# Input and memory handed over in both layouts, one column block for index keys, low rank and head weights, router in column groups

## The chip, the cores and the metric

The kernel runs on one core of one Trainium2 chip. The metric is the device time of one execution in microseconds; of several executions the median is taken. The core has TensorE (PE, matrix products; PEld is its weight load), VectorE (DVE), ScalarE (ACT), GpSimd (POOL) and SyncE (SP), which here issues nearly all DMAs.

## The reference, cut to what matters

A decoder trunk of two layers on 256 tokens of 1024 features, with a memory of 256 tokens, all float32. `hn` is RMSNorm of the stream `h`.

```
z = hn @ W_in[i]                        # 2616 columns, cut into the groups below
(a_q, a_k, a_v, a_g, a_lr, b_u, c_q, c_k, c_v, c_qi, c_ki, c_wi, d_uv) = split_cols(z, IN_SPLITS)
# widths: 128 128 256 256 16 256 256 256 256 256 32 8 512
o_a: gated linear attention;  logit = a_lr @ wa2 + ba        (a_lr: 16 columns, the low rank)
o_b: causal pooling of b_u
o_c: sparse attention; score = sum_h relu(c_qi_h . c_ki) * c_wi_h, top 64 of the visible tokens
     (c_ki: 32 columns, the index key; c_wi: 8 columns, one weight per index head)
o_d: chunked gating of d_uv
h += concat(o_a, o_b, o_c, o_d) @ W_out[i]
h += cross_attention(RMSNorm(h), RMSNorm(mem)) # keys and values from mem @ wkv, gain norm_mem
h += SwiGLU(RMSNorm(h))                        # layer 0
h += top-2-of-8 SwiGLU experts                 # layer 1: logits = RMSNorm(h) @ router (1024 x 8)
```

One final RMSNorm ends it.

## The kernel before, in words

Everything is written out by hand: one instruction list for each engine, ordered by semaphores. There is no planner. Each engine runs its list in order, so whatever stands behind a waiting instruction on the same engine waits too. One `for layer in range(2)` loop in each list holds the layer; the expert stage comes behind it.

**Weights.** Seven ring slots of 2 MB (`ring`) hold the weights. They are packed on the host into the order in which they are used, and SP issues one DMA per unit as soon as the slot's semaphore `slot_free` says that PE is done with what was there. `IN_UNITS` names the seven column blocks of `W_in`: unit `U_QI` holds index queries, index keys and head weights (296 columns), `U_A` the first 512 columns, `U_AG` the gate and the low rank (272 columns). Then `U_CQ`, `U_CV`, `U_BU`, `U_UV` follow, and after them `wkv`, `W_out` in four parts, `wq` and `wo`.

**Features on partitions.** PE contracts over the partitions, so the normalised stream is needed transposed, as `xnT` (128 partitions, 8 feature tiles, 256 tokens). `transposes()` (line 1574) gets it by 16 float32 products of `h` with `diag`, a diagonal matrix of 1/rms that DVE makes in `factors()` (lines 1014, 1015); each product shows as two records in the profile. `normed_out()` on DVE (line 1023) and ACT (line 690) then copies PSUM to `xnT` times the gain, which stands in `pcol`, one column per tile. `pcol` is itself made each layer: eight small DMAs fill `prow` (lines 517 to 521), PE transposes it (line 1633) and ACT copies it (line 723). The memory goes the same way in layer 0: `memr` (which lies in `memT`) is squared by ACT, multiplied with `diag` by PE, and copied back to `memT`.

**The start of a layer on PE.** Transposes of `h`; index queries (two column tiles of 128, `on_features`, line 1588, 8 products of 256 tokens each); index keys (32 columns, one more such group); head weights on tokens (`on_tokens`, line 1593: 8 products for each of two token tiles with 8 moving columns); in layer 0 the bias product (line 1649); in layer 0 three filler products (`keep_busy`, line 1560), in layer 1 the first column tile of `U_A`; the index scores `dots(1, 256)` (line 1658, eight products in four row groups); in layer 0 the transposes of the memory and three more fillers; transposes of `wsr` (line 1676); `U_A` (lines 1588, 1593); in layer 0 two products for the relative bias (line 1693) from `hank`, which comes back from DRAM by a DMA that POOL issues (line 620); `dots(0, 128)`; the low rank (16 columns, 8 products, line 1588); the gate on tokens (line 1593); then `U_CQ`, the `logit` product (line 1713) between its two halves, and the rest of the units.

**DVE in the same stretch.** After `xnT`: masks `wsr`, copies `qiT`, in layer 0 makes the memory's factors and half of the copies, then `score_and_take(1, 256)` and `score_and_take(0, 128)`: eight multiply-adds each (line 1092) and eight rounds of maximum and replace (lines 1099, 1100). Only behind these stands the copy `lrT` of the low rank (line 1067), for which the `logit` product waits.

**The router.** After the last update of `h` in layer 1 PE turns `h` by 16 products with the identity (line 1990), ACT and DVE scale it (lines 865, 1355), PE forms the logits of 8 experts in one accumulation of 8 products (line 1997), ACT copies them, two transposes (line 2002) bring them on tokens, and DVE makes the choice. The expert stage then streams 2 MB units through ring slots and two extra buffers; the first units are loaded ahead while the router runs.

Of the kernel before, what the change touches and what calls it, by code (L numbers as in the profile page):

```python
# [8 lines left out]
P = 128  # L9
# [4 lines left out]
ALU = mybir.AluOpType  # L14
# [50 lines left out]
def packed_blocks():  # L65

    for layer in range(DEPTH):
        for s, (lo, hi) in enumerate(IN_UNITS):
            yield ("in_units", layer, s), "w_in", layer, (0, D), (lo, hi)
        yield ("wkv", layer), "xa_wkv", layer, (0, D), (0, 2 * GW)  # L70
        for i, m in enumerate(WOUT_ORDER):
            yield ("wout", layer, i), "w_out", layer, (256 * m, 256 * m + 256), (0, D)
        yield ("wq", layer), "xa_wq", layer, (0, D), (0, GW)
        yield ("wo", layer), "xa_wo", layer, (0, GW), (0, D)
    for c, n in enumerate(FFN_TILES):
        f0 = P * sum(FFN_TILES[:c])
        for w, name in enumerate(("ffn_w1", "ffn_w3")):
            yield ("ffn", 3 * c + w), name, 0, (0, D), (f0, f0 + n * P)
        yield ("ffn", 3 * c + 2), "ffn_w2", 0, (f0, f0 + n * P), (0, D)
# [7 lines left out]

def pack_weights(inputs):

    return np.concatenate([rows_on_partitions(inputs[name][index, r0:r1, c0:c1])  # L90
                           for _, name, index, (r0, r1), (c0, c1) in packed_blocks()])

def pack_experts(inputs):
# [11 lines left out]
    return out  # L106

# [63 lines left out]
IN_UNITS = ((C_QI, C_UV), (0, 512), (C_AG, C_BU), (C_CQ, C_CV), (C_CV, C_QI), (C_BU, C_CQ), (C_UV, IN_W))  # L171
# [10 lines left out]
for _key, _, _, (_r0, _r1), (_c0, _c1) in packed_blocks():  # L182
    PACKED[_key] = (_at, _at + (_r1 - _r0) * (_c1 - _c0))
    _at = PACKED[_key][1]
# [4 lines left out]

CONST = {}  # L190
_at = 0
for _name, _w in (("ident", P), ("vis", 256), ("reset", 256), ("bd", 256), ("tril", P), ("inv", 512),
                  ("before", P), ("ones", P), ("iota", P), ("eidx", 8), ("erev", 8), ("limit", 16)):
# [5 lines left out]
def shape_constants():  # L199
# [21 lines left out]
    put("erev", 8 - np.arange(8)[None, :])  # L221
    put("limit", np.concatenate(([SMALL], np.full(N_EXP - 1, SMALL - 1), [SMALL + P], np.full(N_EXP - 1, P)))[None, :])
# [14 lines left out]
def build(nc, A, out):  # L237
    ctx = ExitStack()
    with ctx:
# [76 lines left out]
        wa2 = sb("wa2", [GLA_RANK, P])  # L316
        prow = sb("prow", [N_ROWS, P])
        pcol = sb("pcol", [P, N_ROWS])
# [47 lines left out]
        memr = memT[:, :, :].rearrange("p k m -> p (k m)").rearrange("p (t d) -> p t d", t=2)  # L366
# [7 lines left out]
        lrT = qidx[0:GLA_RANK, 768:1024]  # L374
# [1865 lines left out]
```

## Time and profile before

| | us |
|---|---|
| median of 3 runs | 1389.37 (1389.14 to 1391.38) |
| profiled execution | 1391.46 |
| its span | 1389.7 |
| PE busy | 1286.5 (93%) |
| DVE busy | 484.4 (35%) |
| ACT busy | 373.7 (27%) |
| POOL busy | 79.9 (6%) |
| moved by DMA | 433.51 MB, 312 GB/s over the span |

The profiled execution took 2.1 us more than the median. The profile of it has several views: the busy time of the engines in slices, the chain of work that ended last (each piece is what the next one had waited for), the instructions in order of time, groups of instructions by line, and the DMA issues with the time to landing.
### The profile page before, as it was taken

Reading aid. Unit: us, or ns where it says so; the run is one execution under the profiler, and the core shown is the slowest. Engines: PE = TensorE matmul, PEld = TensorE weight load, DVE = VectorE, ACT = ScalarE, POOL = GpSimd, SP = SyncE. Lnnn points to the kernel's source line nnn. Section 1 sums busy time; section 2 is a strip of 40 time slices with the busy share of each in tenths; the row PEclk is TensorE's granted clock in tenths of the full one; section 3 lists DMA queues with packets and bytes.
Section 4 is the critical chain, followed back from the end, with each engine's and each line's share of the span. In section 5 each row is a group of like instructions: output and inputs, shape, how many; then the busy total and the mean of one; then the engine's idle time right before and its main releaser. Section 6 shows DMA issues by size and latency. Waiting matters only on the chain.

```text
span 1389.7 us, 15762 instructions
## 1 busy us (share of the span) xinstructions
PE 1286.5 (93%) x6338; PEld 785.7 (57%) x6338; DVE 484.4 (35%) x819; ACT 373.7 (27%) x574; POOL 79.9 (6%) x68
## 2 busy tenths in 40 slices
PE   7999999999999999999989879779779778999996
PEld 5777888888888688634323224224224225788532
DVE  1627267777626453600101001001001004988102
ACT  2244154444323423301101001001001005776102
POOL 0263000000004600000000000000000000000000
PEclk9999999999999999999999999999999999999998
DMA  9431633443181308799999999999999999999895
GB/s 361 177 116 37 231 133 137 177 186 137 40 352 65 117 1 365 306 417 428 427 428 426 429 428 430 428 428 427 430 429 428 429 427 430 427 428 379 365 428 244
DMA packets 37416, 433.51 MB, mean 312 GB/s; under 512 B 5726, under 2 KB 7924, under 8 KB 9588
## 3 DMA queue, kind: packets, MB, share of 16 engines
q1 hardware_dynamic: 37172, 432.25, 75.4%
q8 instruction: 37, 0.61, 0.2%
q0 software_dynamic: 192, 0.53, 0.1%
q14 instruction: 15, 0.12, 0.0%
HBM read 431.71 MB, written 1.05 MB: 311 GB/s over the span
## 4 chain that ended last, share of the span: by engine, by line
PE 62%; DMA 32%; DVE 4%; ACT 1%; issue 1%; SPq 0%; DVEq 0%; ACTq 0%
DMA ring<-in_experts 31%; PE bank L2089 10%; PE bank L2169 9%; PE bank L1588 8%; PE bank L1975 6%; PE bank L1593 5%; PE bank L2099 5%; PE bank L1611 4%; PE bank L1979 3%; PE bank L1574 1%; PE bank L1865 1%; PE bank L1866 1%; PE bank L1872 1%; PE bank L2022 1%; PE bank L2047 1%; PE bank L1560 1%
## 5 line engine op out<-in xcount | busy, mean ns | idle before, releaser
L2089 PE MATMUL bank<-ring,xs 128*64 128x512 f32 x1552 | 352.1, 597 | 41.2 <-DMA ring<-in_experts 41.2
L2089 PEld LDWEIGHTS bank<-ring,xs 128*64 128x64 f32 x1552 | 109.6, 137 | 247.9 <-issue 228.4
L2099 PE MATMUL bank<-ring,s_act 128*64 128x512 f32 x768 | 176.3, 597 | 34.5 <-DMA ring<-in_experts 34.3
L1477 DVE TENSOR_TENSOR s_act<-wsT,bank 128x256 f32<-128x256 f32 x49 | 20.6, 421 | 510.8 <-ACT wsT L903 510.8
L2099 PEld LDWEIGHTS bank<-ring,s_act 128*64 128x64 f32 x768 | 55.6, 137 | 142.8 <-issue 131.4
L1975 PE MATMUL bank<-x_both,wf_hi 128*128 128x512 f32 x336 | 118.9, 396 | 0.0
L903 ACT ACTIVATE wsT<-bank 128x256 f32<-128x256 f32 x49 | 18.8, 383 | 336.3 <-PE bank L2047 336.3
L1588 PE MATMUL bank<-xnT,ring 128*128 128x256 f32 (+2 forms) x448 | 102.5, 388 | 0.6 <-ACT bias L752 0.6
L1501 DVE TENSOR_TENSOR ring_lo<-ring,w_hi 128x2048 fp32r<-128x2048 f32 (+1 forms) x44 | 96.0, 2193 | 20.2 <-ACT w_hi L960 20.2
L838 ACT ACTIVATE wf_hi<-ring 128x1024 fp32r<-128x1024 f32 x66 | 69.8, 1060 | 98.6 <-PE bank L1975 67.5
L1979 PE MATMUL bank<-x_both,wf_lo 128*128 128x256 f32 x336 | 94.1, 280 | 0.0
L1272 DVE TENSOR_TENSOR wf_lo<-ring,wf_hi 128x1024 fp32r<-128x1024 f32 x66 | 80.5, 1223 | 33.4 <-ACT wf_hi L838 33.4
L1588 PEld LDWEIGHTS bank<-xnT,ring 128*128 128x128 f32 (+2 forms) x448 | 80.5, 182 | 18.5 <-issue 2.1
L960 ACT ACTIVATE w_hi<-ring 128x2048 fp32r<-128x2048 f32 (+1 forms) x44 | 80.7, 1839 | 34.6 <-PE bank L2169 29.8
L899 ACT ACTIVATE j_act<-bank 128x512 f32<-128x512 f32 x49 | 29.3, 597 | 191.4 <-PE bank L2089 191.4
L1593 PE MATMUL bank<-ring,xnT 128*128 128x256 f32 (+2 forms) x320 | 78.5, 400 | 0.0
L2169 PE MATMUL bank<-w_hi,xg 128*128 128x512 f32 x224 | 72.8, 402 | 2.6 <-DVE xg L1508 2.6
L1975 PEld LDWEIGHTS bank<-x_both,wf_hi 128*128 128x128 f32 x336 | 63.1, 188 | 14.9
L1593 PEld LDWEIGHTS bank<-ring,xnT 128*128 128x128 f32 x320 | 56.4, 193 | 20.9 <-issue 16.0
L1979 PEld LDWEIGHTS bank<-x_both,wf_lo 128*128 128x128 f32 x336 | 63.5, 189 | 0.9
L2169 PEld LDWEIGHTS bank<-w_hi,xg 128*128 128x128 f32 x224 | 42.9, 192 | 13.7 <-issue 3.5
L2047 PEld LDWEIGHTS bank<-cst,j_act 128*128 128x128 f32 x224 | 24.0, 141 | 40.9 <-issue 40.1
(361 smaller groups left out, 1459.8 us busy)
## 6 DMA issues: line engine op xcount, KB each, us to landing
ring<-in_experts SPq DMA_DIRECT2D x166, 2048.0 KB, 29.2
ring<-in_packed SPq DMA_DIRECT2D x18, 1536.0 KB, 6.9
ring<-in_packed SPq DMA_DIRECT2D x11, 2048.0 KB, 10.2
ring<-in_packed SPq DMA_DIRECT2D x16, 1024.0 KB, 4.9
extra<-in_experts SPq DMA_DIRECT2D x2, 2048.0 KB, 11.8
ring<-in_packed SPq DMA_DIRECT2D x2, 1184.0 KB, 6.1
ring<-in_packed SPq DMA_DIRECT2D x2, 1088.0 KB, 10.9
h<-in_x SPq DMA_DIRECT2D x2, 512.0 KB, 4.0
```

The lines of the kernel that those rows point to most:

```text
L838: act.activation(as_piece(w, ffn_hi(i)), weights, ACT.Copy).then_inc(S["hi_ready"], 1)
L960: act.activation(w_hi[:, i % NB, 0:hi - lo], ring[:, slot, lo:hi], ACT.Copy)\
L1272: dve.tensor_tensor(as_piece(w, ffn_lo(i)), weights, as_piece(w, ffn_hi(i)), sub)\
L1501: dve.tensor_tensor(ring_lo[slot][:, lo:hi], ring[:, slot, lo:hi], w_hi[:, i % NB, 0:hi - lo], sub).then_inc(S["lo_ready"], 1)
L1588: i = mm(dst, w[:, k, :], src[:, k, :], start=k == 0, stop=k == KT - 1)
L1593: i = mm(dst, src[:, k, P * t:P * t + P], w[:, k, :], start=k == 0, stop=k == KT - 1)
L1611: ins = mm(dst, x, y, start=opens and n % 3 == 0, stop=closes and n % 3 == 2)
L1975: ins = mm(dst[:, :], wh[:, k, :], x_both[:, k, :], start=k == 0, stop=False, skip_group_check=True)
L1979: ins = mm(dst[:, 0:SEQ], wl[:, k, :], x_both[:, k, 0:SEQ], start=False, stop=k == KT - 1, skip_group_check=True)
L2089: i = mm(ps[d % 2][SMALL * side:SMALL * side + SMALL, :], xs[:, k, :], weights(u)[:, at:at + FC], start=k == 0, stop=k == KT - 1)
L2099: i = mm(ps[6 + half][SMALL * side:SMALL * side + SMALL, :], s_act[:, d % 4, x + side, :], weights(u)[:, at:at + FC], start=d == 0 and x = ...
L2169: ins = mm(dst[:, :], st_, mv, start=opens, stop=closes)
```

## The change

Three things, in one edit:

1. `x` and `mem` also come from the host with features on partitions (`xT`, `memT`), and the gains come as a ready `columns` tensor (128 x 2 x 41) for both layers. In layer 0 PE multiplies a matrix of ones with `diag`, which puts 1/rms of each token on all partitions, and DVE multiplies `xnT` in place by gain and factor (eight instructions); for `mem` ACT copies the factors and POOL multiplies `memT` in place. The `prow` loads, their transposition and the transposes of `x` and `mem` go. Layer 1 still transposes `h`.
2. Index keys, low rank and head weights stand side by side in `U_QI` (columns 256 to 328, with 16 zero columns), so one group of 8 products yields all three; two small transposes bring the head weights on tokens. The low rank leaves `U_AG`, and DVE copies it ahead of the scores.
3. The router's turn of `h` uses transposes, and its products go to four column groups of the array, two of 32 columns at a time; a product with a matrix `parts` adds the four parts and transposes.

Around this, loads and waits are moved: in SP's order the rest of the constants goes behind the parameters, and `mem` behind `U_A`; ACT waits for the first small loads before it starts; the first half of `U_A` takes the place of the fillers in layer 0 as well; the memory's squares follow the first relu on ACT.

```diff
-IN_UNITS = ((C_QI, C_UV), (0, 512), (C_AG, C_BU), (C_CQ, C_CV), (C_CV, C_QI), (C_BU, C_CQ), (C_UV, IN_W))
+QUADRANT = 32
+AT_LR, AT_WI = QUADRANT, 2 * QUADRANT
+IN_UNITS = (((C_QI, C_WI), (C_LR, C_BU), (None, AT_WI - AT_LR - GLA_RANK), (C_WI, C_UV)),
+            ((0, 512),), ((C_AG, C_LR),), ((C_CQ, C_CV),), ((C_CV, C_QI),), ((C_BU, C_CQ),), ((C_UV, IN_W),))
@@ SP @@
-            sp.dma_start(ident, consts[:, 0:P]).then_inc(S["loaded_cst"], 16)
-            sp.dma_start(cst[:, P:CONST_W], consts[:, P:CONST_W]).then_inc(S["loaded_cst"], 16)
+            sp.dma_start(cst[:, 0:2 * P], consts[:, 0:2 * P]).then_inc(S["loaded_first"], 16)
+            sp.dma_start(columns[:, :, :], A["columns"]).then_inc(S["loaded_first"], 16)
+            sp.dma_start(xnT[:, :, :], A["xT"]).then_inc(S["loaded_xT"], 16)
...
-                    sp.dma_start(prow[row:row + n, :], A[name][lay].rearrange("e (r c) -> (e r) c", c=P))\
-                      .then_inc(S["loaded_prow"], 16)
...
+                            sp.dma_start(cst[:, 2 * P:CONST_W], consts[:, 2 * P:CONST_W]).then_inc(S["loaded_cst"], 16)
+                    if s == U_A:
+                        if layer < 1:
                             sp.dma_start(memr, A["mem"][0].rearrange("(t p) d -> p t d", p=P))\
                               .then_inc(S["loaded_mem"], 16)
+                            sp.dma_start(memT[:, :, :], A["memT"]).then_inc(S["loaded_mem"], 16)
@@ POOL @@
+            gp.wait_ge(S["xT_a"], count(0, 2, 2, 2))
+            gp.tensor_tensor(memT[:, :, :], memT[:, :, :], rs_mem.unsqueeze(1).broadcast_to([P, KT, MEM]), ALU.mult)\
+              .then_inc(S["xT_v"], 2)
@@ ACT @@
             act.wait_ge(S["zeroed"], 1)
+            act.wait_ge(S["loaded_first"], 32)
...
                 i.then_inc(S["rel"], 1)
                 if layer < 1:
-                    normed_out(layer, 2, memT, None, 4)
+                    act.wait_ge(S["loaded_mem"], 64)
+                    for t in range(TT):
+                        root_mean(memr, bias[:, :, :].rearrange("p h x -> p (h x)"), t)
@@ DVE @@
+                if layer < 1:
+                    dve.wait_ge(S["loaded_xT"], 16)
+                    dve.wait_ge(S["xT_ps"], count(layer, norm_no(layer, 0), 4, 4))
+                    for kt in range(KT):
+                        i = dve.scalar_tensor_tensor(xnT[:, kt, :], xnT[:, kt, :], pcol[layer][:, R_MIX + kt:R_MIX + kt + 1],
+                                                     ps[0][:, 0:SEQ], mult, mult)
...
+                group("ki")
+                dve.tensor_copy(wiT, ps[5][AT_WI:AT_WI + IDX_HEADS, 0:256])
+                dve.tensor_copy(lrT, ps[5][AT_LR:AT_LR + GLA_RANK, 0:256]).then_inc(g_ev["lr"], 1)
+                dve.wait_ge(S["wi_ps"], L1)
...
                     dve.memset(st[:, 95:96], 0.0).then_inc(S["scored"], 1)
+                    if t and layer < 1:
+                        factors(layer, 2)
...
-                out_of("lr", lrT, ps[4][0:GLA_RANK, 0:256])
@@ PE @@
+            def factors_on_columns(layer, no, bank):
+
+                for t in range(TT):
+                    pe.wait_ge(S["diag_ready"], count(layer, no, 2, t + 1))
+                    mm(ps[bank][:, P * t:P * t + P], cc("ones"), diag[:, t, :], start=True, stop=True)\
+                        .then_inc(S["xT_ps"], 2)
...
-                transposes(layer, norm_no(layer, 0), h, busy=(4 if layer else 0, 0))
+                if layer < 1:
+                    factors_on_columns(layer, norm_no(layer, 0), 0)
+                else:
+                    transposes(layer, norm_no(layer, 0), h, busy=(4, 0))
...
-                on_features(ps[5][0:32, 0:256], w[:, :, 256:288])
-                for t in range(TT):
-                    i = on_tokens(ps[5][:, 256 + 8 * t:264 + 8 * t], w[:, :, 288:296], t)
-                i.then_inc(g_ps["ki"], 1)
+                on_features(ps[5][0:AT_WI + IDX_HEADS, 0:256], w[:, :, 256:256 + AT_WI + IDX_HEADS]).then_inc(g_ps["ki"], 1)
...
-                if layer < 1:
-                    keep_busy(6, 3)
-                else:
-                    pe.wait_ge(arrived[U_A], landed[0])
-                    on_features(ps[6][:, 0:256], w_in(U_A)[:, :, 0:P])
+                pe.wait_ge(arrived[U_A], landed[0])
+                on_features(ps[6][:, 0:256], w_in(U_A)[:, :, 0:P])
                 pe.wait_ge(g_ev["qi"], L1)
                 pe.wait_ge(g_ev["ki"], L1)
                 dots(1, 256).then_inc(S["dots_ps"], 1)
-                if layer < 1:
-                    pe.wait_ge(S["bias_row"], 1)
-                    transposes(layer, 2, memr, 4, then_all=True)
-                    keep_busy(6, 3)
-
+                pe.wait_ge(g_ev["lr"], L1)
+                for t in range(TT):
+                    i = pe.transpose(ps[5][:, 256 + IDX_HEADS * t:256 + IDX_HEADS * (t + 1)], wiT[:, P * t:P * t + P],
+                                     ident[AT_WI:AT_WI + IDX_HEADS, AT_WI:AT_WI + IDX_HEADS])
...
-                on_features(ps[4][0:GLA_RANK, 0:256], w[:, :, 256:272]).then_inc(g_ps["lr"], 1)
...
-                    i = mm(xT(kt)[:, P * t:P * t + P], h[:, t, P * kt:P * kt + P], ident, start=True, stop=True)
+                    i = pe.transpose(xT(kt)[:, P * t:P * t + P], h[:, t, P * kt:P * kt + P], ident)
...
-                i = mm(ps[4][0:N_EXP, 0:SEQ], routw[:, kt, :], xnT[:, kt, :], start=kt == 0, stop=kt == KT - 1)
+            for q in (0, 2):
+                for b in (q, q + 1):
                     normed(1, norm_no(1, 2), b)
+                for x in range(2):
+                    for b in (q, q + 1):
+                        i = mm(ps[4][QUADRANT * b:QUADRANT * b + N_EXP, 0:SEQ], routw[:, 2 * b + x, :], xnT[:, 2 * b + x, :],
+                               start=x == 0, stop=x == 1, tile_position=(0, QUADRANT * b))
...
-                i = pe.transpose(ps[5][:, N_EXP * t:N_EXP * t + N_EXP], lgT[:, P * t:P * t + P], ident[0:N_EXP, 0:N_EXP])
+                i = mm(ps[5][:, N_EXP * t:N_EXP * t + N_EXP], lgT[:, P * t:P * t + P], cc("parts")[0:LG_ROWS, :],
+                       start=True, stop=True)
```

## Rows read from the trace of the kernel before

**Rows 1.** The page's slices of 34.7 us: what the DMAs moved.

```profile
GB/s 361 177 116 37 231 133 137 177 186 137 40 352 65 117 1 365 306 417 428 427 428 426 429 428 430 428 428 427 430 429 428 429 427 430 427 428 379 365 428 244
```

**Rows 2.** Chain of waits, first 100 us: start us, us, what.

```profile
4.96 4.68 DMA prow<-in_sgu_b
...
10.60 5.74 PE bank L1574 x32
16.34 10.52 PE bank L1588 x48
26.85 3.67 PE bank L1593 x32
...
31.25 2.33 PE bank L1560 x6
33.59 1.86 PE bank L1658 x16
...
42.29 0.44 PE bank L1676 x4
...
59.53 3.61 PE bank L1588 x16
```

**Rows 3.** Instructions in order of time, from the start to 60 us.

```profile
1.43 1.28 ACT L707 ACT_TABLE_LOAD   x1 [1.43 <-POOL zeros L612]
...
5.31 0.36 SPq L532 DMA_DIRECT2D ring<-in_packed  x1
5.64 1.06 ACT L680 ACTIVATE r<-h 128x1024 f32<-128x1024 f32 x1 [2.71 <-DVEq L1036]
...
8.18 0.29 ACT L681 ACTIVATE st<-st,eps 128x1 f32<-128x1 f32 x1
...
39.94 0.71 POOL L620 DMA_DIRECT2D vx<-bias_scratch  x1
```

**Rows 4.** DMA issues of the first 100 us: size, median us to landing.

```profile
ring<-in_packed SPq DMA_DIRECT2D x1, 1184.0 KB, 7.1
...
vx<-bias_scratch POOLq DMA_DIRECT2D x1, 256.0 KB, 8.7
```

**Rows 5.** Busy time by stretch, with granted clock (PEclk), DMA share, GB/s.

```profile
31.70:35.10 3.40, 3.40 (x21) 2.19 (x19) 0.45 (x2) 3.31 (x9) 0.77 (x1) 0.51 1.01 422
403.90:407.30 3.40, 3.40 (x12) 2.95 (x13) 0.00 (x0) 1.67 (x5) 0.00 (x0) 0.50 0.95 395
575.00:580.00 5.00, 5.00 (x24) 2.04 (x24) 3.23 (x14) 1.13 (x3) 0.00 (x0) 1.00 0.00 0
```

**Rows 6.** Chain of waits, start of layer 1.

```profile
386.76 3.62 PE bank L1574 x32
...
400.90 4.24 PE bank L1593 x32
405.13 6.34 PE bank L1588 x16
411.47 1.12 PE bank L1658 x16
```

**Rows 7.** Instructions in order of time, layer 1: the low rank's copy.

```profile
438.03 0.41 DVE L1067 COPY qidx<-bank 16x256 f32<-16x256 f32 x1
438.59 0.67 PE L1713 MATMUL bank<-qidx,wa 16*128 16x256 f32 x2 [0.32 <-DVE qidx L1067]
```

**Rows 8.** The router: one row in order of time, then two of the chain.

```profile
559.83 1.71 ACT L865 ACTIVATE xnT<-bank,pcol 128x256 f32<-128x256 f32 x4
...
560.66 3.55 PE bank L1997 x16
...
564.84 0.23 PE bank L2002 x2
```

**Rows 9.** Products in two column halves of one bank, in order of time.

```profile
123.96 0.43 PE L1809 MATMUL bank<-zeros,gla 128*64 128x256 f32 x1
123.97 0.43 PE L1809 MATMUL bank<-Sst,gla 128*64 128x256 f32 x1
```

**Rows 10.** By line: durations min/median/max in ns.

```profile
L1284 DVE SCALAR_TENSOR_TENSOR x_both<-bank,pcol,x_both x8: 476/476/478, 199.8 to 202.6; 128x256 fp32r<-128x256 f32 x8
L646 POOL TENSOR_TENSOR ring_lo<-ring,ring_lo x4: 4509/4516/4520, 87.5 to 461.0; 128x2048 fp32r<-128x2048 f32 x4
```

More of the change, by code:

```diff
@@ L106, in pack_experts, with pack_columns, features_on_partitions @@
     return out
+def pack_columns(inputs):
+    out = np.empty((DEPTH, N_ROWS, P), np.float32)
+    for name, row, n in (("norm_mix", R_MIX, 8), ("norm_xa", R_XA, 8), ("norm_mem", R_MEM, 8), ("norm_ffn", R_FFN, 8),
+                         ("gla_ba", R_BA, 1), ("pool_b", R_PB, 2), ("pool_scale", R_PS, 2), ("sgu_b", R_SB, 4)):
+        out[:, row:row + n] = inputs[name].reshape(DEPTH, n, P)
+    return np.ascontiguousarray(out.transpose(2, 0, 1))
+def features_on_partitions(rows):
+    return rows_on_partitions(np.ascontiguousarray(rows[0].T)).reshape(P, KT, -1)
 def slot_of(u):
@@ L315, in build @@
         pwbd = sb("pwbd", [P, 2, P])
-        wa2 = sb("wa2", [GLA_RANK, P])
-        prow = sb("prow", [N_ROWS, P])
-        pcol = sb("pcol", [P, N_ROWS])
+        wa2 = sb("wa2", [AT_LR + GLA_RANK, P])[AT_LR:AT_LR + GLA_RANK, :]
+        columns = sb("columns", [P, DEPTH, N_ROWS])
+        pcol = [columns[:, layer, :] for layer in range(DEPTH)]
         routw = sb("routw", [P, KT, N_EXP])
@@ L749, in _ @@
                 if layer < 1:
+                    act.wait_ge(S["xT_ps"], count(layer, 2, 4, 4))
+                    act.activation(rs_mem, ps[3][:, 0:MEM], ACT.Copy).then_inc(S["xT_a"], 2)
                     act.wait_ge(S["hank_ps"], 1)
@@ L1564, in normed, with transposes @@
                 pe.wait_ge(S["xT_a" if b % 2 else "xT_v"], count(layer, no, 2, b // 2 + 1))
-            def transposes(layer, no, src, bank0=0, busy=(0, 0), then_all=False):
+            def transposes(layer, no, src, bank0=0, busy=(0, 0)):
                 keep_busy(2, busy[0])
@@ L1571, in transposes @@
                     for kt in range(KT):
-                        if not isinstance(no, int) and t == 0 and kt == KT - 2:
-                            pe.wait_ge(S["pcol_done"], layer + 1)
                         i = mm(xT(kt, bank0)[:, P * t:P * t + P], src[:, t, P * kt:P * kt + P], diag[:, t, :],
@@ L1681, in _ @@
                 w = w_in(U_A)
[L1682 to L1684 removed]
+                on_features(ps[6][:, 256:512], w[:, :, P:2 * P]).then_inc(g_ps["a"], 1)
+                pe.wait_ge(S["bias_row"], 1)
                 for t in range(TT):
@@ L1688, in _ @@
                 if layer < 1:
+                    pe.wait_ge(S["rel"], first)
+                    factors_on_columns(layer, 2, 3)
                     pe.wait_ge(S["bias_hank"], 32)
```

153 lines of the change are left out of this document (71 added, 82 removed).

## The prediction

> **What bounds the kernel now.** I read the slices first: from slice 18 on the DMAs move about 428 GB/s almost to the end [rows 1], so the expert stage, half of the run, is a stream of weights at its ceiling. The change leaves that stream alone. What it can do is let it begin earlier. The stream waits for PE: between 575 and 580 us nothing is moved and PE is busy all the time [rows 5], because all units that fit are loaded and no slot is free until the first job's products run. So whatever the stages ahead save on PE moves the whole expert stage forward, and nothing is kept back by the stream.
>
> Then the chain of waits at the two places that are edited. In layer 0 it is a DMA wait for the last small gain load until 9.64 us and from there PE, with few breaks [rows 2]. In layer 1 it is PE as well, and one group of 16 records takes 6.34 us where 48 such records took 10.52 us in layer 0 (0.22 us each) [rows 2, 6]: the granted clock there is 0.50, that is 1.2 GHz [rows 5]. The clock fell in both layers right behind the 32 records with 8 moving columns (L1593) [rows 2, 5, 6]. So PE is the bound, and its price has three parts: records, waits, and the clock that thin work takes away.
>
> **Layer 0, the start.** Before, the squares of x run from 5.64 to 8.47 us (2.83) [rows 3], PE turns x in 5.74 us and the index queries begin at 16.34 [rows 2]. Now:
> - ACT waits for the first constants and the columns, and only then loads its table: that load, 1.28 us, stood beside the x load and now stands in the path. The two small loads are the third and fourth issue. They land no sooner than x (5.6, [rows 3]) and no later than the last gain load did, which stood behind a megabyte more (9.6, [rows 2]); I take 6.5, nearer to x, since what stands ahead is little. Squares: 6.5 + 1.3 + 0.2 + 2.8 = 10.8.
> - Factors on DVE 0.5, two products on PE 0.4: 11.7. DVE then has eight instructions of the form of L1284, 0.476 us each: 3.8 in all, a pair each 0.95 [rows 10], and PE starts behind the first pair, at 12.7.
> - The weights of U_QI landed at 5.31 + 7.1 = 12.4 [rows 3, 4]. A megabyte of xT goes ahead and 0.9 MB of constants behind; the block itself grows by 0.13 MB. Some 0.25 MB net at 0.35 MB/us gives 13.1 to 13.3. So PE starts at 13.3; the bounds are 12.7 and 15.5 (small loads at 9.6).
> - PE is cold. The 32 records of the turn took 5.74 us here and 3.62 in layer 1 [rows 2, 6]: 2.1 us lost, which is 4.2 us at half clock. That stretch now falls on the index queries, so again 2.1 us are lost: 13.3 + 10.5 + 2.1 = 25.9 for queries and the joint group (it is 48 records as before, a group of 72 columns costs what one of 32 does, since 256 columns move). Before: 26.85. Gain 0.9. This is where 5.7 us of turning bring little.
>
> **Layer 0, what follows.** The head weights on tokens go: 3.7 [rows 2]. From 31.25 to 42.29 (11.0 us) PE had fillers, scores at low clock (1.86 where layer 1 has 1.12), the turn of the memory, a wait and fillers [rows 2, 6]; of this the scores stay: 11.0 - 1.1 = 9.9 gained. The first half of U_A that now stands there is work moved, not added. The low rank's group goes: 3.6 (59.53, [rows 2]). Added on PE: two transposes for the head weights, 0.11 each by L1676: 0.2 [rows 2]; two products of ones for the memory, four records of 0.11 (3.62 / 32) [rows 6]: 0.45. One wait: the bias comes back by POOL's DMA, issued at 39.94 and landed 8.7 later, 17.4 us after the bias product's end at 31.25 [rows 2 to 4]. That product now ends at 25.9 + 0.7 = 26.6, so the data is there at 44.0. PE has by then done U_A's first half 3.5, scores 1.1, head weights 0.2, wsr 0.4 to 0.6, and 48 records of U_A (10.4): it arrives at 42.9. Wait 1.1, bounds 0 and 5 (the loads are at their ceiling longer, with 1 MB more of memory). Behind it stand the second scores and all that follows. Sum for layer 0: 0.9 + 3.7 + 9.9 + 3.6 - 0.2 - 0.45 - 1.1 = 16.3.
>
> At no cost I count: the key copies on ACT, 1.5 us, beside U_A's first half (3.5, the cover that before were fillers); the low rank's and head weights' copies on DVE, at the same place; the memory's squares, 2.8 us on ACT behind the relu, and its factors on DVE (1 us between scores and choice), both beside U_A; POOL's multiplication of memT, of the size of L646, 4.5 us [rows 10], beside choice and projections, from about 44 us on, while PE reads memT just ahead of the products at 124 us before, some 108 now [rows 9]. If POOL's cover went it would cost those 4.5. The loads of all units are issued in the same order, and end some 3 us later (1 MB of xT, 1 MB of memT), while PE comes 16 us earlier. By the slices (361, then 177 GB/s) the first block's loads ended near 50 us; at 59.5 PE had five of seven units still ahead [rows 1, 2]. I count 0, upper bound 3.
>
> **Layer 1.** The head weights and the slow group end at 411.47, having begun at 400.90: 10.6 us for the 32 thin records and 16 records of U_A [rows 6]. Without the thin ones the clock has no reason to fall, and U_A's 16 records cost 16 x 0.22 = 3.5. Gain 7.1, of which 2.9 is clock. The low rank's group goes: 3.6 as in layer 0. PE's idle of 0.32 before the logit product, behind the choice on DVE and the copy (438.03), goes since the copy stands ahead of the scores now [rows 7]; 0.3. Added 0.2. The pcol transposition is hidden behind the squares. The scores and the choice, 25 us on ACT and DVE from 412.6 to the copy at 438.0 [rows 6, 7], become late relative to PE by some 3 us; next on DVE is the sum for the gate, whose reader on PE, the attention product, stands 17 us of products behind the logit product. Sum: 7.1 + 3.6 + 0.3 - 0.2 = 10.8; bounds 8 (the clock falls elsewhere for as long) and 11.
>
> **Router.** The turn halves, but it wasn't last: ACT can scale only after the second tile's square, at 559.83, and ends at 561.54 [rows 8]. PE started the logits at 560.66 and took 3.55. Now the last two column groups wait until 561.6. Whether they run side by side shows in products in two column halves of a bank, which start 10 ns apart [rows 9]: four products of 0.44 then take 0.9 and end at 562.5 instead of 564.2, 1.7 gained. One after another they would end at 564.2, 0 gained. Adding the parts is four records where 0.23 us were two [rows 8]: +0.2. I take 1.4, bounds -0.3 and 1.6. Beyond it the DVE's choice of experts follows directly.
>
> PE's work here becomes thin: 16 transposes, gaps, and products with 8 columns. In this trace thin records took the clock to 0.50 for 3.4 us in layer 0 and 6.8 in layer 1 [rows 5, 6]. If that happens here, the four paired products and what follows cost up to 3.5 us more (another 3.57 us of gather stand behind the choice). The Trainium skill speaks for it, in "TensorE: Matmul & The Clock Gate", Part 4 on PE-mode transpose: a transpose does not count as busy in the way a product does, so the full clock is not held by it. No row here shows transposes alone long enough to tell.
>
> **Sum.** 16.3 + 10.8 + 1.4 = 28.5 us. The profiled execution (1391.46 with a span of 1389.7) would take 1363.0; it lies 2.1 us above the median of 1389.37, from which 28.5 gives 1360.9. I say 1361.
>
> **Rivals.**
> 1. The router goes at half clock. For it: the thin records' effect in both layers. Against it: the fillers that stay. Router gain 1.4 becomes -2 to -1: 1364.
> 2. The start is bound by loads: the small columns land as late as the gain load did, and the bias's way through DRAM is slow under 2 MB more of traffic. Queries start 2.2 later (15.5), the wait is 5 instead of 1.1: 6.1 less, 1367.
> 3. The change doesn't do what it says in column groups: they run in turn. 1.7 less: 1362.6, within the range.
> 4. The other side: the fillers and the full products were what held the clock. Without them PE stands at 1.2 GHz through the projections of layer 0 and part of layer 1. Work at half clock takes twice its time, so it decides from 28.5 us of work (57 us at half clock) on; if half of the some 70 us of PE's work between 13 us and the end of layer 0's projections ran so, 35 us would be lost: 1396. Against it: the stretch is dense, and the before had 3.4 and 6.8 us at half clock [rows 5, 6], right behind the thin records that go.
> 5. The expert stream gives part of the gain back, because the loads ahead of it are late and its first jobs then wait. Half lost: 1375. Against it: the 5 us without a DMA [rows 5].
>
> **Numbers.** Forecast with rival 3: 0.72; rival 1: 0.10; rival 2: 0.12; rival 4: 0.02; rival 5: 0.04. The range goes from 1357 (all upper bounds) to 1367, which takes in rivals 1 and 2. A measurement of this kernel tells 0.2%, 2.8 us, from no change. Faster by more: 0.97; within: 0.01; slower: 0.02.
>
> **What would show it.** Gate products on tokens (L1593 at 63.14 before) start near 46.8; layer 1 from the first query product to the logit product is 10.8 shorter, with a granted clock of 1.00 throughout; no L1574 in layer 0; the router's products end some 2 us after ACT's scaling begins. I am wrong if the clock is 0.50 anywhere in layer 0 beyond the first 18 us, if the expert stream's first 5 us pause grows, or if PE waits over 2 us for the bias.

## The result and the profile after

The changed kernel took 1368.2 us (median of 4 runs, 1365.22 to 1369.12), the kernel before in the same comparison 1390.4 (1389.14 to 1393.55): a ratio of 0.9836, 95% interval 0.9815 to 0.9857. It is faster, by 22 us instead of the forecast 28.5, and the time lies 1.2 us above the range that was given. The profiled execution took 1365.22 us, the fastest of the four, with a span of 1363.4.

Where the time went is read from the starts of six pieces of work in the two profiles. The last column is what the forecast says.

| stretch (us) | before | after | gain | forecast |
|---|---|---|---|---|
| start to the gate's products on tokens | 63.07 | 51.24 | 11.8 | 16.3 |
| from there to the turn of layer 1 | 323.53 | 323.47 | 0.1 | 0 |
| turn of layer 1 to the logit product | 51.99 | 40.89 | 11.1 | 10.8 |
| from there to the router's turn | 118.34 | 118.53 | -0.2 | 0 |
| router's turn to the first expert product | 19.18 | 17.77 | 1.4 | 1.4 |
| expert stage and end | 813.6 | 811.5 | 2.1 | 0 |

Only the first row falls short of the forecast, by 4.5 us. The 2.1 us of the last row were not forecast; that stage varies by 3 us between profiles (last section). The six gains add up to the 26.3 us between the two spans. That is more than the 22 us of the medians, since the profiled execution of the kernel before lay above its median and that of the kernel after below. In the first row's stretch, the chain of waits of the kernel after (start us, us, what) answers to [rows 2]:

```profile
2.10 4.21 DMA columns<-in_columns
...
6.47 1.28 ACT L743
...
12.24 0.88 DVE xnT L1106 x2
...
13.26 13.31 PE bank L1633 x48
...
28.14 0.49 ACT gla L765
...
29.26 6.24 DMA bias_scratch<-gla
...
36.56 9.98 DMA vx<-bias_scratch
...
46.59 3.40 PE bank L1730 x4
...
50.50 0.60 ACT bias L784
...
51.24 3.91 PE bank L1638 x17
```

The chain runs through no product between 26.6 and 46.6 us: it is the bias on its way through DRAM, and PE, busy with U_A in the meantime, arrives first and waits. In order of time, PE alone and ACT's bias copies:

```profile
42.87 0.61 PE L1625 MATMUL bank<-diag,cst 128*128 128x128 f32 x4
...
46.59 2.08 PE L1730 MATMUL bank<-kxT,glab 128*128 128x512 f32 x2 [3.12 <-DMA vx<-bias_scratch]
...
48.46 1.51 PE L1730 MATMUL bank<-vx,glab 128*128 128x512 f32 x2
...
49.90 0.73 PE L1698 MATMUL bank<-qidx 32*128 32x128 f32 x16
50.01 1.08 ACT L784 ACTIVATE bias<-bank 128x512 f32<-128x512 f32 x2 [6.05 <-PE bank L1730]
51.24 1.10 PE L1638 MATMUL bank<-ring,xnT 128*128 128x256 f32 x4 [0.61 <-ACT bias L784]
```

A wait of 3.12 us, two pairs of products that take 2.08 and 1.51, and 0.61 for ACT's copies. In the kernel before, the same pairs took 1.02 each, with no wait ahead of them; the 0.61 stood there too:

```profile
56.38 1.02 PE L1693 MATMUL bank<-kxT,glab 128*128 128x512 f32 x2
57.24 1.02 PE L1693 MATMUL bank<-vx,glab 128*128 128x512 f32 x2
...
59.53 0.81 PE L1588 MATMUL bank<-xnT,ring 128*16 128x256 f32 x3 [0.61 <-ACT bias L752]
```

The stretches with the granted clock (columns as in [rows 5]) say why the products are slow:

```profile
13.20:18.70 5.50, 5.44 (x13) 4.39 (x14) 2.55 (x8) 0.00 (x0) 0.00 (x0) 1.00 1.13 367
18.70:26.50 7.80, 7.80 (x38) 5.84 (x37) 1.30 (x5) 0.00 (x0) 0.00 (x0) 1.00 0.99 413
42.50:46.60 4.10, 0.98 (x8) 0.74 (x6) 3.82 (x13) 0.89 (x2) 2.47 (x1) 0.93 1.01 416
46.50:49.40 2.90, 2.81 (x4) 1.18 (x4) 2.64 (x5) 0.00 (x0) 2.13 (x1) 0.50 0.97 412
374.70:415.70 41.00, 40.99 (x231) 35.00 (x231) 23.22 (x76) 10.82 (x24) 3.64 (x7) 1.00 0.75 308
```

```profile
374.71 3.84 PE bank L1615 x32
378.55 13.82 PE bank L1633 x64
392.36 1.07 PE bank L1698 x16
...
415.67 0.62 PE bank L1753 x2
```

No thin group (records with 8 moving columns) is there, and the 16 records of U_A cost 13.82 / 64 x 16 = 3.5 us. The router, in order of time, answers to [rows 8]:

```profile
537.03 1.55 ACT L897 ACTIVATE xnT<-bank,columns 128x256 f32<-128x256 f32 x4
...
538.00 1.77 PE L2039 MATMUL bank<-xnT,routw 128*8 128x256 f32 x16 [1.24 <-ACT xnT L897]
```

The same 16 records took 3.55 us in one accumulation; now they fit into 1.77, half: the column groups run beside each other.

### The profile page after: what moved, and what is told of

Its sections match the earlier page's. It is cut to its first block, busy times and chain, and to the rows that moved or that the text cites. A ratio compares the mean times of both kernels' runs of the same rounds, so it can differ in the third digit from the quotient of the medians.

```text
span 1363.4 us, 15394 instructions
## 1 busy us (share of the span) xinstructions
PE 1254.3 (92%) x6158; PEld 760.4 (56%) x6158; DVE 487.4 (36%) x823; ACT 370.1 (27%) x563; POOL 84.9 (6%) x69
## 4 chain that ended last, share of the span: by engine, by line
PE 61%; DMA 34%; DVE 2%; ACT 2%; issue 1%; SPq 0%; DVEq 0%; POOL 0%; ACTq 0%; POOLq 0%
DMA ring<-in_experts 32%; PE bank L2133 10%; PE bank L2213 9%; PE bank L1633 7%; PE bank L2016 6%; PE bank L1638 5%; PE bank L2143 5%; PE bank L1656 4%; PE bank L2020 3%; PE bank L1906 1%; PE bank L1913 1%; PE bank L1907 1%; PE bank L2066 1%; PE bank L2091 1%; PE bank L1615 1%
## 5 line engine op out<-in xcount | busy, mean ns | idle before, releaser
L1544 DVE TENSOR_TENSOR ring_lo<-ring,w_hi 128x2048 fp32r<-128x2048 f32 (+1 forms) x44 | 95.8, 2193 | 18.7 <-ACT w_hi L992 18.5
L1633 PE MATMUL bank<-xnT,ring 128*128 128x256 f32 (+1 forms) x416 | 95.0, 388 | 1.1 <-DVE xnT L1106 1.1
L1633 PEld LDWEIGHTS bank<-xnT,ring 128*128 128x128 f32 (+1 forms) x416 | 78.6, 191 | 15.1 <-DMA ring<-in_packed 1.4
L1638 PE MATMUL bank<-ring,xnT 128*128 128x256 f32 (+1 forms) x256 | 70.4, 433 | 0.6 <-ACT bias L784 0.6
L1638 PEld LDWEIGHTS bank<-ring,xnT 128*128 128x128 f32 x256 | 48.5, 190 | 20.2 <-issue 15.1
## 6 DMA issues: line engine op xcount, KB each, us to landing
extra<-in_experts SPq DMA_DIRECT2D x2, 2048.0 KB, 12.7
```

The lines of the kernel that those rows point to most:

```text
L1544: dve.tensor_tensor(ring_lo[slot][:, lo:hi], ring[:, slot, lo:hi], w_hi[:, i % NB, 0:hi - lo], sub).then_inc(S["lo_ready"], 1)
L1633: i = mm(dst, w[:, k, :], src[:, k, :], start=k == 0, stop=k == KT - 1)
L1638: i = mm(dst, src[:, k, P * t:P * t + P], w[:, k, :], start=k == 0, stop=k == KT - 1)
```

## The experiments

All on the kernel after unless said otherwise. "Gate" is the start of the gate's products on tokens in the profile (51.24 in the kernel after), "layer 1" the time from the first query product to the logit product (37.2; 48.4 before). In the first four the kernel before took 1391.2 (9 runs).

**The kernel after again, unchanged** (`again`).

> The changed kernel once more, with nothing changed, to see what varies between its executions. Theory A: the missing time of layer 0 is the wait of the bias products for their data from DRAM (3.1 us in the first profile) and the granted clock that falls to 0.50 in it; then this profile shows the wait again, between 2 and 4 us, and a median between 1365 and 1369. Theory B: the first profile (1365.2) was a good draw and the three later runs (1367.4 to 1369.1) have stretches at 1.2 GHz elsewhere; then this profile shows 10 us more at 0.50 than the 8.7 us of the first, in the expert stage or the router.

Measured: 1367.4 us (1365.76 to 1369.33), ratio 0.983 [0.9815, 0.9845]. Gate at 50.72, a wait of 4.1 us for the bias, clock at 0.50 from 48.1 for 3.4 us, layer 1 37.2. The shortfall came again.

**Fillers in the wait** (`fill`), to keep the clock up without shortening the wait:

```diff
                     factors_on_columns(layer, 2, 3)
+                    keep_busy(2, 7)
                     pe.wait_ge(S["bias_hank"], 32)
```

> Seven filler products (3.0 us at full clock) ahead of the wait for the bias data in layer 0. They end when the data lands, so the wait itself is not shortened. Theory A with both parts, wait and clock: the four records of the bias products take 1.7 us instead of 3.4, 1.7 us less than the changed kernel. Rival, the wait alone costs and the clock nothing: no change within 0.5 us. If the fillers end late, up to 1 us is given back.

Measured: 1365.8 us (1362.89 to 1366.61), ratio 0.9817 [0.9802, 0.9832]. Its chain:

```profile
42.40 0.44 PE bank L1625 x4
42.84 3.02 PE bank L1603 x14
45.86 1.78 PE bank L1731 x4
...
48.16 0.60 ACT bias L784
...
48.90 7.14 PE bank L1638 x32
```

No half clock in layer 0, the bias products in 1.78 us instead of 3.40 or 2.60, gate at 48.9, which is 1.8 us ahead of `again` and 2.3 ahead of the kernel after. Not all of that is the clock: the data landed at 45.6 here, 1.2 and 0.9 us sooner than there. From the start of the bias products to the gate it took 3.04 us, against 3.88 and 4.65, so the clock is worth 0.8 to 1.6 us. The medians differ by 1.6 us, as expected, but their intervals overlap.

**The bias products behind the gate's** (`late`), so that nothing waits for the bias:

```diff
-                    pe.wait_ge(S["bias_hank"], 32)
-                    pe.wait_ge(S["ws_done"], 1)
-                    for i2 in range(2):
-                        i = mm(ps[4 + i2][:, :], glab[:, 0:P], hank[i2][:, :, :], start=True, stop=True)
-                    i.then_inc(S["hank_ps"], 1)
...
-                pe.wait_ge(S["bias_done"], 1)
                 w = w_in(U_AG)
                 for t in range(TT):
                     i = on_tokens(ps[5][:, 256 * t:256 * t + 256], w[:, :, 0:256], t)
                 i.then_inc(g_ps["ag"], 1)
+                if layer < 1:
+                    pe.wait_ge(S["rel"], second)
+                    pe.wait_ge(S["bias_hank"], 32)
+                    for i2 in range(2):
+                        i = mm(ps[2 + i2][:, :], glab[:, 0:P], hank[i2][:, :, :], start=True, stop=True)
+                    i.then_inc(S["hank_ps"], 1)
```

ACT's bias copies go behind its copy of the gate, and the attention product waits for them.

> The bias products of layer 0 stand behind the gate products instead of ahead of the second scores, in banks 2 and 3, and ACT's copies of them behind the gate's. The data lands at 46.6, PE gets there at about 51. Theory A: wait 3.1, slow products 1.7 and PE's stop for ACT's copies 0.6 all go, 5.4 us less: 1363 where the changed kernel has 1368. Rival (the lost time of layer 0 lies in the start, before 27 us): 0 to 1 us less, since the start is untouched.

Measured: **1360.25 us** (1360.04 to 1362.16, 5 runs), ratio 0.9781 [0.9768, 0.9794], 7.2 us below the unchanged kernel beside it (1367.4); the expectation was 5.4 us less. Its chain and one stretch:

```profile
42.79 0.73 PE bank L1699 x16
43.52 7.10 PE bank L1639 x32
50.62 1.72 PE bank L1744 x4
52.34 3.45 PE bank L1634 x16
```

```profile
42.50:55.00 12.50, 12.21 (x66) 10.00 (x67) 11.51 (x39) 4.33 (x9) 7.03 (x7) 1.00 1.01 422
```

The gate starts at 43.52, 7.7 us (7.2 against `again`) before the kernel after. Of these, 1.72 are the bias products, which now come behind, and 1.3 (0.6) an earlier end of the query products, which this edit doesn't touch. So 4.7 to 4.9 us in the profile hung on the wait, near the expected 5.4 and the size of the miss in the first row. It is the place, the price and the cause of the miss, and the version that beats both kernels. What the median gained beyond that, some 2 us, this profile doesn't explain.

**ACT's table load ahead of its wait** (`table`): one more activation before ACT waits for the small loads.

```diff
             act.wait_ge(S["zeroed"], 1)
+            act.activation(st[:, 93:94], eps[:, :], ACT.Sqrt)
             act.wait_ge(S["loaded_first"], 32)
```

> ACT loads its table (1.28 us) and runs one tiny activation before it waits for the small loads, so that the squares start 1.5 us earlier. If the start is bound by the chain of squares and factors: 1.5 us less. If the weights of the first unit bound it as soon as the chain is shorter (issued at 3.2, landed 9.7 later, 12.9): PE starts at 12.9 instead of 13.3, 0.4 us less. The cold stretch moves along in both cases.

Measured: 1366.7 us (1365.4 to 1367.74), ratio 0.9821 [0.9806, 0.9836], not to be told from `again`. The queries started at 13.13 us instead of 13.26, since PE then waited 1.3 us for the weights of U_QI, and the gate at 51.08. In the kernel after the chain of squares and factors ended last, and the weights, issued at 3.2 and 9.7 us on their way, had landed some 0.2 us earlier. So the two bind the start almost together, and a shorter chain gains 0.1 us.

**Both of these** (`late_table`), in a second comparison with 9 runs of the kernel before at 1391.1:

> The bias products behind the gate's products (as in `late`) and ACT's table load ahead of its wait for the first small loads (as in `table`). Theory (the query products start when U_QI has landed, at about 13.0 us, so the earlier table load brings nothing once the stall for the bias is gone): the time of `late`, 1360.2, within 1. Rival (the 0.1 to 0.8 us that `table` took less than the kernel after were real): 1359.5 or less, with the query products starting below 12.9 us.

Measured: 1360.2 us (1357.94 to 1362.76), ratio 0.9777 [0.976, 0.9795], the queries at 13.18. The table load brings nothing here either.

**Fillers ahead of the first products** (`warm`), on top of `late_table` (they run between 6.5 and 13.5 us):

```diff
+            def warm_up(n):
+                for _ in range(n):
+                    mm(ps[2][:, 0:P], ident, cc("ones"), start=True, stop=True)
...
                 for t in range(TT):
+                    if bank == 0:
+                        warm_up(1 if t else 4)
...
                     factors_on_columns(layer, norm_no(layer, 0), 0)
+                    warm_up(6)
```

> As `late_table`, and PE runs eleven filler products of 128 columns between about 8 and 13 us, in the waits ahead of the query products. Theory (TensorE was idle before and stands at 1.2 GHz for its first 4 to 5 us of work, which cost the kernel after some 2 us of its query products): full clock is recorded from 13 to 14 us instead of 16 to 18, the queries and the joint group take 10.7 us instead of 12.6, and the time is 2 us below `late_table`, 1358. Rival (short work with gaps does not raise the clock, or it falls again in the wait for the weights): full clock from 16 us or later, the same time as `late_table`, 1360.

Measured: 1359.8 us (1359.45 to 1361.04), ratio 0.9774 [0.9759, 0.9788]. The chain:

```profile
10.93 2.56 PE bank L1626 x12
13.49 10.57 PE bank L1642 x48
```

Full clock from 13.6 us, and the 48 records take 10.57 us instead of 13.22 in `late_table`: the mechanism is as stated. Layer 1 began at 367.48, against 369.84 in `late_table` and 368.67 in `late`. Yet of these 1.2 to 2.4 us only 0.4 shows in the median, well inside the intervals. The profile's expert stage was 1 us longer than in `late_table` (814.5 against 813.5), which is within what that stage varies by (below). Whether `warm` is worth 2 us in the median stays open.

**x turned by PE again in layer 0** (`x_undone`); the transposed x isn't loaded, DVE and ACT scale as in layer 1.

```diff
-            sp.dma_start(xnT[:, :, :], A["xT"]).then_inc(S["loaded_xT"], 16)
...
-                if layer < 1:
-                    factors_on_columns(layer, norm_no(layer, 0), 0)
-                else:
-                    transposes(layer, norm_no(layer, 0), h, busy=(4, 0))
+                transposes(layer, norm_no(layer, 0), h, busy=(4 if layer else 0, 0))
```

> The kernel after, but in layer 0 PE turns x again by 16 products with the diagonal matrix (DVE and ACT scale them), and the transposed x is not loaded; everything else stays, the ready gains too. Theory (the turn only moves the cold stretch of TensorE off the query products, and without its megabyte the weights land some us earlier): turn from 10 to 16 us, queries start at 16 to 16.9 and take 10.6 instead of 12.6, so the gate starts 1 to 1.6 us later and the time is 1 to 1.6 us above the unchanged kernel, 1368.5. Rival (the turn was 5.7 us on the path and the change took it all away): 5 us more, 1372.

Measured: 1367.5 us (1365.66 to 1368.07, 4 runs), ratio 0.982 [0.9801, 0.984]: the same as with the edit. Its chain at the start:

```profile
10.06 6.25 PE bank L1604 x32
16.31 10.38 PE bank L1622 x48
```

The queries and the joint group end at 26.69, in the kernel after at 26.57. Taking 6.25 us of products off the start brought 0.1 us in these two profiles: the queries began 3.05 us sooner and took 2.93 longer. Those products had been the ones that ran cold; now the query products do (13.31 instead of 10.38). In the kernels with the same start as the kernel after and no fillers in it, that end varies from 25.3 to 28.1 us. So a gain of about 1 us isn't excluded, nor by the medians; one of 5 us, the rival, is. The gate started at 52.17, 0.9 to 1.4 us later than in the kernel after and `again`, about what the theory said, yet for another reason: the way of the bias took 19.8 us here.

**Thin records in layer 1, four ways.** The prediction put the half clock of layer 1 before [rows 5, 6] down to the 32 thin records. `thin` puts them back alone, between queries and joint group; `fat` runs eight filler products of 256 columns there instead.

```diff
+                if layer:
+                    for t in range(TT):
+                        on_tokens(ps[7][:, 8 * t:8 + 8 * t], w[:, :, 256:264], t)
                 on_features(ps[5][0:AT_WI + IDX_HEADS, 0:256], w[:, :, 256:256 + AT_WI + IDX_HEADS]).then_inc(g_ps["ki"], 1)
```

> The kernel after with the head weights' two groups on tokens (8 moving columns, 32 records) put back in layer 1 alone, between the query products and the joint group; their result goes to a free bank and isn't read. Theory of the prediction (thin records take the clock down): 3.7 to 4.2 us for the records and a stretch of 3.4 to 6.8 us at 0.50 behind them, 1.7 to 3.4 us more, so that layer 1 from the first query product to the logit product is 5.4 to 7.6 us longer than 37.2. Rival (another thing took the clock down in the kernel before, the thin records cost their own time only): 3.7 us longer, clock 1.00 throughout.

> At the place of `thin`, eight filler products of 256 columns (16 records) in layer 1 instead, of nearly the same length. Theory of the prediction: 3.5 us longer than 37.2 from the first query product to the logit product, clock 1.00 throughout. Rival (any added work there does the same as thin records): a stretch at 0.50 here as well, 5 us or more.

Both gave layer 1 in 40.7 us, clock 1.00 (single profiles; 1366.4 and 1372.1 us in one run each). In this profile the thin records alone cost their own 3.5 us and no clock, so the prediction's reason for the half clock did not hold as stated. In the kernel before, a group with 32 output columns stood right ahead of them. Three more kernels: `narrow_thin` has that group and the thin records, `thin_twice` 64 thin records, `narrow` the group alone.

```diff
+                    on_features(ps[7][0:32, 0:256], w[:, :, 256:288])
```

> The kernel after with, in layer 1 between the query products and the joint group, first a group of 32 output columns (16 records, as the index keys of the kernel before) and then the 32 thin records; neither result is read. Theory A (both together, some 7 us of work that uses little of the array, took the clock down in the kernel before): a stretch at 0.50 right behind, and layer 1 from the first query product to the logit product 37.2 + 3.5 + 3.5 + 3 = 47 us. Rival B (it was something else of the kernel before): 44.2 us, clock 1.00.

> At the same place 64 thin records (8 moving columns, 6.9 us) and no narrow group. Theory A1 (the length of work with little in it decides, whichever kind): a stretch at 0.50, 47 us. Theory A2 (the narrow group is what matters): clock 1.00, 37.2 + 6.9 = 44.1 us.

> At the same place the group of 32 output columns alone (16 records). Theory A1 (length decides): 37.2 + 3.5 = 40.7 us, clock 1.00. Theory A2 (the narrow group by itself is enough): a stretch at 0.50 and 42 us or more.

| put back in layer 1 | layer 1, us | added | stretch at 0.50 |
|---|---|---|---|
| nothing (after) | 37.2 | | none |
| 32 thin records (`thin`) | 40.7 | 3.5 | none |
| 32-column group (`narrow`) | 40.9 | 3.7 | none |
| both (`narrow_thin`) | 46.2 | 9.0 | 3.4 us from 389.9 |
| 64 thin records (`thin_twice`) | 49.3 | 12.0 | 10.2 us from 391.5 |

Stretches of `thin` (its 32 thin records, then what follows), then of `thin_twice` (its first 35 thin records, then the other 29 and what follows), and the chain's piece with the 64:

```profile
382.90:386.40 3.50, 3.50 (x34) 3.50 (x33) 0.69 (x1) 0.00 (x0) 0.00 (x0) 1.00 1.02 426
386.40:396.00 9.60, 9.60 (x60) 7.53 (x59) 1.01 (x3) 2.98 (x8) 0.00 (x0) 1.00 1.02 423
```

```profile
387.80:391.50 3.70, 3.70 (x36) 3.70 (x35) 0.69 (x1) 0.00 (x0) 0.00 (x0) 1.00 1.00 418
391.50:401.70 10.20, 10.20 (x41) 8.55 (x41) 0.00 (x0) 0.00 (x0) 0.00 (x0) 0.50 0.61 259
```

```profile
387.83 10.01 PE bank L1638 x64
```

PE is busy all through each of them, so this fall is not one of idle time. Either kind alone left the clock; with the two together, or twice the thin kind, it fell. The two together are the kernel before's sequence, and the change removed both kinds, by widening the 32-column group to 72 and by taking the thin records out. In all three kernels with a fall in layer 1 it came while thin records still ran: 2.9 us after the first of them in the kernel before, 3.3 in `narrow_thin`, 3.7 in `thin_twice` (in layer 0 of the kernel before, 1.2 us after the last of them). In `thin` they were over after 3.5 us. These are single profiles and the differences are small. That the 32-column group is needed isn't shown: `thin` could have missed the fall by where its records happened to lie. Why the fall lasted 6.8 us in the kernel before and 3.4 in `narrow_thin` stays open too.

**The router, edit by edit**, each a single profile. `groups_undone` has one accumulation of eight products and two transposes, `turn_undone` the turn by products with the identity, `router_undone` both:

```diff
-                    i = pe.transpose(xT(kt)[:, P * t:P * t + P], h[:, t, P * kt:P * kt + P], ident)
+                    i = mm(xT(kt)[:, P * t:P * t + P], h[:, t, P * kt:P * kt + P], ident, start=True, stop=True)
```

> The kernel after with the router's products in one accumulation of eight and two transposes behind it; the turn of h stays a transposition. Theory (the column groups run side by side and save what the prediction counted, 1.7 less 0.2): from the first router product to the end of the logits 1.5 to 1.8 us longer, router turn to first expert product 19.2 to 19.5 us instead of 17.8. Rival (the gain in the router came from the turn by transposes): 17.8.

> The kernel after with h turned by products with the identity ahead of the router; the column groups stay. Theory (ACT's square of the second tile ends last, so the turn is hidden): router turn to first expert product 17.8 us, as in the kernel after. Rival (the turn is on the path): 2 us more, 19.6.

> Both edits of the router undone together. Theory (they add up and are independent): router turn to first expert product as in the kernel before, 19.2 us. Rival (each hides behind the other: the turn matters only once the groups are gone): 20 us or more.

| router's turn to first expert product, us | groups | one accumulation |
|---|---|---|
| turn by transposes | 17.77 | 18.48 |
| turn by products | 17.92 | 19.18 |

With the groups the turn is hidden (0.15). Without them it isn't: 0.70. In `router_undone` the chain goes straight from the turn to the logits,

```profile
537.89 3.57 PE bank L2031 x32
541.47 3.55 PE bank L2038 x16
```

so PE itself was last there, and of the 1.4 us neither edit has a share of its own: the groups bring 1.26 or 0.71, depending on the turn. The expectation for `groups_undone` missed by 0.7 to 1.0 for that reason.

## Why the prediction was right or wrong

**Bound.** Right: what the stages ahead save goes through to the expert stage. The pause of the DMA stream before it did not grow, and from gate to layer 1 and from the logit to the router the times stayed the same within 0.2 us. Rival 5 did not come. Rival 4 did not come either; layer 1 stood at full clock.

**Start.** Right in time (queries at 13.26, forecast 13.3), in part by chance: the prediction had the weights bind and the chain of squares ready at 12.7, while the chain ended at 13.12 and the weights some 0.2 sooner. The small loads landed at 6.31 (forecast 6.5). Queries and joint group ended at 26.57 instead of 25.9, which lies within what this end varies by (25.3 to 28.1). `x_undone` shows the gain of this edit as 0.1 us in two profiles; the forecast for the stretch was 0.9, and the two can't be told apart.

**The wait for the bias: the step that failed.** The prediction put it at 1.1 us, "bounds 0 and 5", and nothing behind it. Step by step in the profile:
- The way through DRAM began 0.6 later (27.2, since the queries ended late) and took 19.4 us instead of 17.4. Up to POOL's second issue it took 9.3 us, from 27.2 to 36.56, where the kernel before had 8.7 (31.25 to 39.94). From that issue to the landing it took 10.0, where the kernel before had 8.7 [rows 4]. Data at 46.59, forecast 44.0: 2.6 us. The prediction carried the 17.4 over although 2 MB more of loads stood in the order, and kept the slower way for the range and rival 2. The slower way is no single draw: in the sixteen profiles other than the kernel before's it took 18.6 to 21.1 us. What differs is the load beside the second transfer: 319 GB/s before, where the loads ran out from 46 us on, and 420 now (the two stretches below the list). That speaks for the traffic, but no run changed it alone. Taking away the megabyte of xT did not help: in `x_undone` the way took 19.8 us, at 424 GB/s. What the megabyte of memT or the changed order does was not tested.
- The price of the wait. The prediction said itself that a fall to 0.50 behind the start would prove it wrong, as a wait of over 2 us would, yet had no term for the fall. The bias products took 3.40 us instead of 1.73. From the data to the gate 4.65 us, forecast 2.8: 1.85 us. Of this 1.7 is the clock. The other 0.2 is the sum itself, since the same pieces, with the stop of 0.61 for ACT's copies among them, took 3.0 in the kernel before (56.55 to 59.53).

```profile
39.94:48.60 8.66, 7.87 (x38) 6.97 (x39) 8.12 (x24) 1.12 (x3) 1.55 (x3) 1.00 0.76 319
```

```profile
36.56:46.55 9.99, 6.91 (x34) 5.95 (x33) 9.28 (x31) 2.15 (x5) 3.73 (x4) 0.97 1.03 420
```

Together 4.45 us, the whole of the row that is short. `fill` shows the clock's part by itself (0.8 to 1.6 us), `late` the wait and the clock (4.7 to 4.9). The mechanism was rival 2's, half of it: the bias's way was slow, the small columns were not. That its 1367 was near is luck: it had no term for the clock either, counted 2.2 us for late queries that did not come and 3.9 for more wait, where 2.0 came.

The term varies from run to run. Eleven profiles have the same order in layer 0 as the kernel after (`again`, `table`, `fat`, `thin`, the three of the router, the three with narrow or doubled thin records, and itself): PE waited 2.4 to 4.7 us for the bias, the gate started at 48.7 to 54.8, and the clock fell in eight of them, for 3.4 or 6.8 us. In the three without a fall the gate started at 48.7, 48.8 and 48.9, in the others at 50.7 or later. The latest, 54.8, had the small columns land at 8.10 and the queries begin at 15.04. A sum made for one order of arrival has to carry such a term with both its values.

**Layer 1.** Right in size: 11.1 against 10.8. The reason for the half clock was at best incomplete: 32 thin records alone left the clock at 1.00, behind a group of 32 output columns they did not, one profile each. As both groups went, the number held either way. Of the gain of 7.1 the clock's part was 3.4 rather than 2.9, because the thin records ran partly at half clock too (4.24 us against 3.67 in layer 0).

**Router.** Right in size, 1.4, and the groups run side by side (rival 3 is out); the clock stayed at 1.00 (rival 1 is out). The Trainium skill's rule in "TensorE: Matmul & The Clock Gate", Part 4, that transposes don't count as busy, cost nothing here: the 16 of them took 1.03 and 1.09 us with products ahead of them and 0.51 us of idle time between, which is too short to say more of it. The reading that the turn "wasn't last" was wrong for the kernel before, where the logits started right behind its 3.57 us (557.09 to 560.66), and right for the kernel after.

**The remaining 1.8 us.** The sum was set against a median of 1389.37 from three runs. Over the next comparisons the kernel before came out at 1391.2, 1391.1 (9 runs each) and 1392.2 (7 runs). From 1391.2 the same 28.5 us would give 1362.7, and with the 4.4 us missing 1367.1, against 1367.4 in `again` and 1368.2 in the first comparison. That is arithmetic on medians that vary by 1 to 2 us, and no run shows it by itself.

## What to carry to other kernels

When a change takes work away in front of a transfer with a long way of its own (here 19 us through DRAM), the transfer becomes late by all that was taken away; price the wait with the clock that can fall in it, and look for a consumer that can be moved behind other work: here that one move was worth 7 us in the median (some 5 in the profile), beside the 22 of the whole change. Removing work from a stretch in which TensorE is cold anyway brings little (0.1 us for 6.25 us of products, in two profiles), because the cold falls on what comes next. And when light groups seem to take the clock down, look at what stands right ahead of them too, and at more than one profile.

## What the runs showed of the hardware

- A wait of 3.1 us on a PE that had been busy since 13 us was enough for the granted clock to go to 0.50, for 3.4 us (6.8 in `table`, `fat` and `turn_undone`, with waits of 3.16 to 3.35), although in `thin` a wait of 3.23 us was not. A longer wait didn't mean a longer fall: 4.73 us in `groups_undone` cost 3.4 us at 0.50.
- The clock also fell with PE 100% busy: 3.7 us into 64 records of 8 moving columns (10.2 us at 0.50) and 3.3 us into 32 such records behind 16 with 32 output columns (3.4 us). Neither 32 thin records nor the 32-column group alone had a fall, in one profile each.
- Eleven short filler products between 6.5 and 13.5 us gave full clock from 13.6 us; the kernels with the same start and without them had it from 16.3 to 20.1.
- The expert stage has a stretch of 3.4 us at 0.50 between 1136 and 1155 us in some executions and not in others. In ten profiles with it the stage took 812.3 to 814.5 us, in six without it 811.5 to 812.6: part of the spread between runs, and one reason why 1 to 2 us could not be settled above.
- 256 KB that POOL loaded back from DRAM landed 8.7 us after the issue in the kernel before, with 319 GB/s moved in that time, and 9.5 to 11.7 us after it in the other sixteen profiles (420 GB/s in the kernel after).
